# Index projection and index scores of a hybrid SSD / sparse-attention layer joined into one stage

## What is computed

```python
h = jnp.einsum('bld,de->ble', x, w_in)            # ... qi (8 x 64), ki (64), wi (8) are columns of it
s = jnp.einsum('bqhd,bld->bqhl', qi, ki_all) * IDX_DIM ** -0.5
score = jnp.einsum('bqh,bqhl->bql', wi * IDX_HEADS ** -0.5, jax.nn.relu(s))
score = jnp.where(admissible[None], score, -jnp.inf)
top_val, top_idx = lax.top_k(score, k_sel)
```

## Time and profile before

| | us |
|---|---|
| median of 3 runs | 3117.87 (3112.76 to 3118.03) |
| span of the profiled execution | 3115.3 |
| index part (both stages), in that execution | 0 to 452.4 |
| of it, projection of the index columns | 0 to 215.6 |
| of it, scores | 219.0 to 452.2 |

### The profile page before, as it was taken

One profiled execution on the slowest core, in us unless ns is written; L12 is line 12 of the kernel. 1 busy time (PEld: TensorE's weight loads), 2 busy tenths in 40 slices (PEclk: granted clock), 3 DMA queues, 4 the chain that ended last, 5 costly groups with the idle time before them and its releaser, 6 DMA issues. The chain is left out here.

```text
span 3115.3 us, 40926 instructions
## 1 busy us (share of the span) xinstructions
PE 2719.6 (87%) x15348; PEld 2279.6 (73%) x15398; DVE 2179.2 (70%) x3768; ACT 1100.6 (35%) x1970; POOL 634.8 (20%) x694
## 2 busy tenths in 40 slices
PE   6879969999998999996577775899999986599998
PEld 4667539999998888996465653667777765488886
DVE  2326999999999999997688855666666655344333
ACT  2215971112221212212544442555554443232222
POOL 0002002333333333433044532211111000000000
PEclk8869989999999999998699987999999998799999
DMA  5320015222225233346412415211110005522221
GB/s 183 134 83 1 1 58 170 87 89 88 87 87 189 88 102 95 97 142 218 177 41 68 122 45 169 72 41 41 31 31 28 21 20 167 186 93 98 92 81 48
DMA packets 177409, 286.03 MB, mean 92 GB/s; under 512 B 27834, under 2 KB 125890, under 8 KB 173382
## 3 DMA queue, kind: packets, MB, share of 16 engines
q1 hardware_dynamic: 157401, 220.56, 22.4%
q0 software_dynamic: 19824, 62.97, 5.4%
HBM read 177.77 MB, written 105.71 MB: 91 GB/s over the span
## 5 line engine op out<-in xcount | busy, mean ns | idle before, releaser
L705 DVE TENSOR_SCALAR_CACHE_REDUCE project_junk<-all_S,project_cand 128x528 bf16<-128x528 f32 (+7 forms) x256 | 370.0, 1445 | 4.8 <-DVE project_cand L730 4.7
L629 PE MATMUL PS<-project_wh,project_xh 128*128 128x256 f32 x1224 | 348.0, 284 | 8.6 <-POOL project_wl L675 5.7
L629 PE MATMUL PS<-project_xh,project_wh 128*128 128x384 f32 (+1 forms) x880 | 317.0, 360 | 37.9 <-DMA project_xl<-x_parts 37.9
L629 PE MATMUL PS<-project_wl,project_xh 128*128 128x256 f32 x1224 | 347.6, 284 | 0.0
L629 PE MATMUL PS<-project_wh,project_xl 128*128 128x256 f32 x1224 | 347.4, 284 | 0.0
L1601 DVE TENSOR_TENSOR attend_ptl<-PS,attend_pth 128x512 fp32r<-128x512 f32 x272 | 186.3, 690 | 186.9 <-ACT attend_pth L1539 186.0
L629 PE MATMUL PS<-project_xh,project_wl 128*128 128x384 f32 (+1 forms) x880 | 316.3, 359 | 0.0
L629 PE MATMUL PS<-project_xl,project_wh 128*128 128x384 f32 (+1 forms) x880 | 316.0, 359 | 0.0
L705 DVE TENSOR_SCALAR_CACHE_REDUCE project_tie<-all_S,project_cand 128x384 bf16<-128x384 f32 (+6 forms) x224 | 315.7, 1409 | 0.0
L675 POOL TENSOR_TENSOR project_wl<-project_raw,project_wh 128x1024 fp32r<-128x1024 f32 x80 | 201.6, 2541 | 240.4 <-ACT project_wh L642 240.4
L1539 ACT CAST attend_pth<-PS 128x512 fp32r<-128x512 f32 x272 | 157.8, 585 | 242.2 <-PE PS L1486 241.2
(11 more groups left out here) (309 smaller groups left out, 6026.8 us busy)
## 6 DMA issues: line engine op xcount, KB each, us to landing
project_raw<-in_w_in SPq DMA_DIRECT2D x80, 512.0 KB, 4.4
featT<-project_st POOLq DMA_DIRECT2D x66, 192.0 KB, 2.2
featT<-project_st POOLq DMA_DIRECT2D x44, 256.0 KB, 2.3
gate_s<-project_st POOLq DMA_DIRECT2D x68, 128.0 KB, 2.1
gate_a<-project_st POOLq DMA_DIRECT2D x68, 128.0 KB, 2.2
x_conv<-all_S SPq DMA_DIRECT2D x8, 1088.0 KB, 5.3
conv_x<-x_conv SPq DMA_DIRECT2D x8, 1088.0 KB, 6.6
ssd_zs<-gate_s SPq DMA_DIRECT2D x17, 512.0 KB, 4.4
```

The lines of the kernel that those rows point to most:

```text
L629: last = nc.tensor.matmul(PS[:, r % 8, 0:w], lhsT, rhs, start=(k == 0 and j == 0), stop=(k == KT - 1 and j == 2))
L705: v.tensor_scalar((junk, tie)[j % 2][:, 0:L], tile_scores(j), th, None, op, ALU.add, accum_out=into[:, j:j + 1]).then_inc(counted, 1)
```

## The change

The two stages become one, `stage_index`, with one list of steps that all engines walk through. What it does:

- The sample chunk is projected first, then the four prompt chunks (`CH`). Its queries go to a buffer of their own (`qsS`); `qs` shrinks to two chunks of 512 tokens in turn.
- A step is a `turn` (transposing one tile), one eighth of a block (`block`, three matmuls), `back`, `cache` (cached keys of one sequence) or `score` (one unit). The function `spread` deals the score units evenly over the steps of something else.
- While chunk 2, 3 or 4 of this order is projected (tokens 512 to 1023, 1024 to 1535, 1536 to 2047), the score units of the chunk before are dealt over its steps from the fourth on: 16, 64 and 96 units. The other 128 units (tiles 12 to 15) are dealt over the 8 cache steps and the 16 sample units, which come last.
- PSUM: turns use two banks (halves of one tile), projection blocks two instead of three, rows back one, scores three instead of eight.
- The cached keys are loaded when the last projection product is done, since they lie where the weights' parts were. The small parameters are loaded right behind the weights and transposed in the very first step.
- The copies of the queries by POOL are made once a head instead of once a unit.

The diff, cut to its core (what ACT and DVE do in each step is as before, in the order of the list):

```diff
+        CH = [CUTS[-1]] + CUTS[:-1]
...
+        def spread(a, u, first):
+
+            out, done = [], 0
+            for i, step in enumerate(a):
+                out.append(step)
+                upto = len(u) * max(i + 1 - first, 0) // max(len(a) - first, 1)
+                out += u[done:upto]
+                done = upto
+            return out
...
+        def project_steps(c):
+            turns = [("turn", order.index(t)) for t in tiles_of[c]]
+            return turns + [("block", c, f, k) for f in range(5) for k in range(KT)]
+        units, steps = [], [("par",)] + project_steps(0) + project_steps(1)
...
+        for c in range(2, NC):
+            us = score_steps(paired([i for t in tiles_of[c - 1] if t >= SEL0 for i in items(t)]))
+            a = project_steps(c)
+            backs = [("back", j) for j in ((0, 1) if c == 2 else (c - 1,))]
+            steps += spread(a[:1] + backs + a[1:], us, 3)
+            ready.append(len(units))
+        steps.append(("back", NC - 1))
+        late_items = paired([i for t in tiles_of[NC - 1] for i in items(t)])
+        sample_items = paired(items(ST))
+        a = [("cache", s) for s in range(NB)] + [("score", i) for i in sample_items]
+        for step in spread(a, [("score", i) for i in late_items], 0):
+            steps += score_steps([step[1]]) if step[0] == "score" else [step]
...
+                sp.dma_start(rows[NB * 3 + 4:, :], b.ins["conv_b"].unsqueeze(0)).then_inc(rows_in, 16)
+                for i in range(3, TILES + 1):
+                    load(i)
+                sp.wait_ge(proj, 5 * NC)
+                sp.wait_ge(x_st, 32 * NC)
+                sp.dma_start(kc[:], b.cache_kidx.rearrange("b (k p) d -> p (b k) d", p=P)).then_inc(kc_in, 16)
...
+                def turn(i):
+                    pe.wait_ge(x_in[i % 3], 16 * (i // 3 + 1))
+                    for j in range(2):
+                        wait(pe, x_lo, 2 * (i - 1) + j + 1)
...
+                def score(n):
+                    (t, c0, w), h = units[n]
+                    c = chunk_of[t]
+                    if n == first_of[c]:
+                        pe.wait_ge(q_lo, 8 * (c + 1))
+                        pe.wait_ge(k_lo, c + 1)
+                    wait(pe, relu_done, n - 2)
+                    out = PS[:, 5 + n % 3, 0:w]
```

More of the change, by code:

```diff
@@ new lines, in items, with paired @@
+        def items(t):
+            return [(t, c, w) for c, w in even_pieces(keys_of(t))]
+        def paired(some):
+            return [(item, h) for i in range(0, len(some), 2) for h in range(IH) for item in some[i:i + 2]]
+        def spread(a, u, first):
[6 more added lines that the diff above has]
+            return out
@@ new lines, in stage_index @@
+        steps.append(("back", NC - 1))
[4 more added lines that the diff above has]
+            steps += score_steps([step[1]]) if step[0] == "score" else [step]
+        last_on = {}
+        before = []
+        for n, (item, h) in enumerate(units):
+            before.append(last_on.get(item, -1))
+            last_on[item] = n
@@ L206, in stage_index_proj, with run, nothing @@
+        def run(par, turn, block, back, cache, score):
+            act = {"par": par, "turn": turn, "block": block, "back": back, "cache": cache, "score": score}
+            for step in steps:
+                act[step[0]](*step[1:])
+        def nothing(*_):
+            pass
         with nc.Block() as block:
@@ L292, in _ @@
+                run(par, turn, block, back, cache, score)
             @block.scalar
@@ new lines, in block @@
+                def block(c, f, k):
+                    if k < KT - 1:
+                        return
+                    n, (c0, w) = 5 * c + f, CH[c]
+                    act.wait_ge(proj, n + 1)
+                    if f < 4:
+                        if f == 0 and c >= 3:
+                            wait(act, sim_ready, ready[c - 2])
+                        for r in range(2):
+                            half = slice(r * ID, (r + 1) * ID)
+                            cp(q_of(c, f, r)[half], PS[half, 2 + n % 2, 0:w]).then_inc(q_hi, 1)
+                    else:
+                        cp(kdw[0:NR, c0:c0 + w], PS[0:NR, 2 + n % 2, 0:w]).then_inc(k_raw, 1)
+                        act.wait_ge(k_raw, c + 1)
+                        for r in range(2):
+                            end = cp(ks[r * ID:(r + 1) * ID, 0, c0:c0 + w], kdw[0:ID, c0:c0 + w])
+                        end.then_inc(k_hi, 1)
@@ new lines, in cache, with score @@
+                def cache(s):
+                    act.wait_ge(kc_turned, s + 1)
+                    act.wait_ge(x_st, 32 * NC)
+                    for r in range(2):
+                        end = cp(kiS[r * ID:(r + 1) * ID, 0, s, 0:PAST], PS[0:ID, s % 2, :])
+                    end.then_inc(kc_hi, 1)
+                def score(n):
+                    (t, c0, w), h = units[n]
+                    act.wait_ge(sim_ready, n + 1)
+                    wait(act, acc_done, n - 3)
+                    nc.scalar.activation(relu[:, n % 4, 0:w], PS[:, 5 + n % 3, 0:w], ACT.Relu, scale=ID ** -0.5
+                                         ).then_inc(relu_done, 1)
@@ L324, in _ @@
+                run(par, turn, block, nothing, cache, score)
             @block.vector
@@ new lines, in cache @@
+                def cache(s):
+                    dve.wait_ge(kc_hi, s + 1)
+                    if s == 0:
+                        for part in range(2):
+                            v.tensor_copy(kiS[:, part, :, PAST:LS], ks[:, part, SEQ:TOK].rearrange(
+                                "p (b t) -> p b t", b=NB)).then_inc(new_done, 1)
+                    for r in range(2):
+                        end = v.tensor_tensor(kiS[r * ID:(r + 1) * ID, 1, s, 0:PAST], PS[0:ID, s % 2, :],
+                                              kiS[0:ID, 0, s, 0:PAST], ALU.subtract)
+                    end.then_inc(kc_lo, 1)
```

430 lines of the change are left out of this document (197 added, 233 removed).

## The result

| | before | after |
|---|---|---|
| median of 4 runs, us | 3115.32 (3112.49 to 3118.03) | 3065.73 (3056.91 to 3068.49) |
| span of the profiled execution | 3115.3 | 3064.5 |
| start of the big projection | 452.5 | 401.5 |
| from there to the end of the span | 2662.8 | 2663.0 |

The ratio is 0.9839, 95% interval 0.9821 to 0.9856: 49.6 us less. The last line of the table says that all of it was won in the index part, and that what follows kept its length in these two executions.

A forecast was written before the change was run, and what follows sets the result against it. The index part was bound by PE in projections, then DVE in prompt scores; seven pieces, each timed by its slowest engine, moved its end from 452.4 to 403 us, saving 49: forecast 3069 us, range 3040 to 3102.

The forecast's parts named there:

- Start, first product at 26: Start of the index part: sample tile first, one tile turned instead of four; first product at 26 instead of 32.2 us.
- Sample chunk, 23.6 us at the lower level: Projection of the sample chunk: 120 matmuls of 128 columns at the lower clock, 23.6 us as before, end 50.
- Chunk 1, gap 11.5, end 92: Tiles 0 to 3, nothing to overlap: gap of 11.5 us (bounds 9 and 14), 30.3 us of products, end 92.
- Chunk 2, gap 12.3, end 141: Second prompt chunk: gap 12.3 us, products 30, 16 score units on PE 6.5; 49 us in all, end 141.
- Cache keys, 9.5 us to DVE's next work, 297: Behind the last product: wait for the cached keys' transfer, 9.5 us with first transposes and roundings, to 297.
- Last part, 102.5 us: 128 late units over 8 cache steps (34 us by DVE) and 16 sample units (68.5 by PE): 102.5 us, to 399.5.
- Each is last in its own half: Last part: DVE limits the cache steps, PE the sample units; three PSUM banks and four buffers can't even that out.
- POOL's copies at nothing: Sample half: POOL's query copies, 11 us in all, cost nothing under DVE's slack of 9.6; without cover up to 11.
- Rival (a), more gain: Chunk gaps filled, last part evened out to 95 us, sample chunk partly at higher clock: 3050 us; chance 0.19.
- Rival (b), jitter with three banks: In-order queues jitter: sample half 82 instead of 68.5 us, cache steps and two chunks lose too: 3099 us; chance 0.18.
- Rival (c), the clock: Short PE stops drop the granted clock to 1.2 GHz; the whole last part there gives 3149 us; chance 0.07.
- Rival (d), no overlap: Queues block each other, parts add up as before, only start and barrier are saved: 3105 us; chance 0.04.

The follow-up runs named there:

- both rebalancing runs: Against the changed kernel: 16 late units ahead of the first cache step, start 400.6 us; two late units per cache step, seven per sample unit, 402.8; unedited 401.5.

## Why the prediction was right

The forecast was 3069 us and the median is 3065.7. The likeliest case came true, in its mechanism and nearly in its sum; by the steps:

- **What bounds the kernel.** The prediction called PE full in slices 1 to 3 of the strip, where it stands at 6, 8 and 7 tenths; full is right for the products alone, and PE idles at the start and between chunks. The sum was made from the stretches and not from the strip, so nothing hangs on it.
- **The question, when the big projection starts.** Right: the rest kept its length to 0.2 us. That it was so near is luck; in the twelve other executions of changed kernels it took 2655.5 to 2665.4 us against 2662.8 before.
- **Start, first product at 26.** 26.3. The small loads landed at 16.99 and not near 20, so the cover over the new first step was wider than thought.
- **Sample chunk, 23.6 us at the lower level.** 24.3 us. The value was right, and the reason I gave for keeping it ("although back to back") was half of it: back-to-back 128-column products did not raise the clock in 24 us, but entered at the higher pace they kept it for the 12.6 us that they need in two executions, and lost it after 2 us in a third. The trace of before had a fourth case that the prediction passed over: its sample chunk was entered at 0.11 us a product and fell to 0.21 after 0.8 us.
- **Chunk 1, gap 11.5, end 92.** Gap 10.5, end 91.0. It would have been 88 where the clock stays up in the gap, as in three of the thirteen rows.
- **Chunk 2, gap 12.3, end 141.** Gap 14.2, end 140.9: the gap is 1.9 longer, the products with their units are 35.7 instead of 36.5, and chunk 1 had given 1 us.
- **Chunk 3, gap 13.3, end 207.** Gap 13.1, products with units 50.6 for 52.5; end 204.6.
- **Chunk 4, gap 14.5, 80.5 in all, end 287.5.** 79.8 in all; end 284.4. PE is full and DVE close behind (58.9 of 65), as predicted.
- **Cache keys, 9.5 us to DVE's next work, 297.** From 284.4 to 294.9: 10.5 us, the hole that was forecast.
- **Last part, 102.5 us.** 105.1, to the last score at 400.0. Here two terms are mis-sized in opposite directions. The cache half is 31.5 for 34: DVE makes 38 score units in it and not 42, the others are still in the buffers when PE begins its first sample unit, so these 2 us only moved on. The sample half is 73.6 for 68.5. PE takes 71.2 us for it, and a sample unit with its 5.3 late ones 4.4 us and not 4.3. The widths are as priced (67 of its 86 late units are 512 wide, 0.44 us on the mean), and with six banks such a step takes 59.6 / 14 = 4.26 us, so what the price left out is PE's waits with three banks. Behind PE's last matmul the last relus and multiply-adds take 2.3 us more; I had put these into the drain, which is 1.5 us instead of 3.5.
- **"Each is last in its own half."** Right as read from the stretches; the hope that follows from it, a gain by moving units, is not (both rebalancing runs).
- **POOL's copies at nothing.** Right, shown by tripling them.
- **Rival (a), more gain.** Not seen: gaps, last part and sample clock stayed. Its mechanisms are real only in part: the sample clock is worth 11 us where it holds, the gaps 2, evening out the last part nothing so far.
- **Rival (b), jitter with three banks.** Seen with three at some 2 us in the sample half, not at the 13.5 that it was priced at there. My reason against it, that PE leads by some 4 us of DVE work, does not hold, since with two banks the same reasoning gave 2 to 8 us and 29 came. Three banks was right by one bank.
- **Rival (c), the clock.** Granted 1.00 in chunks 3 and 4 and in the sample half, and also with two banks and four times the waits. In the cache half it was 0.88, under the 0.9 that was named as a sign of being wrong, and 0.95 from the last product to 400 us; DVE is the last engine in the cache half, so no time is seen to be lost by it.
- **Rival (d), no overlap.** Excluded; undoing the overlap costs 30 us in the chunks and 19 in the last part.

The misses of single terms (-3 in chunks 3 and 4, +1 at the cache keys, +2.6 in the last part, -2 in the drain) cancel in part, so the sum is better than its terms, and that part of its precision is luck. The clock ahead of chunk 1 could have put the start some 3 us earlier, too.

## What to carry to other kernels

Where one stage fills one engine and the next fills another, price the fusion piece by piece with the pace of each engine per step, and ask at what time the first untouched stage starts; such a sum held within 2 us over 400. Moving work between pieces pays only the price on the engine that is last where it is taken away, and costs the price on the engine that is last where it is put. A busy share of 100% does not say that an engine's waits are free: compare the length of a step that repeats, with one buffer fewer and with many more, and the granted clock in the same stretch. An unchanged total can hide a gain and a loss. And before a gain is put down to an edit, look where in the chain it appears: 3 us of one run here stood ahead of everything that the edit touched.

## What the runs showed of the hardware

- A stream of 128-column products does not reach the higher level of the clock by itself in 24.3 us. Entered at the higher pace, it kept it for its 12.6 us in two executions and lost it in two, after 2 us and, in the kernel before, after 0.8 us. The granted clock's column read 1.00 from 20 to 52 us of the changed kernel while products started every 0.21 us; the pace of the instructions was the surer sign.
- With the same steps ahead of it, the granted clock fell in the gap before chunk 1 in some executions and not in others, which is worth 1.9 us in the products behind it.
- Of PSUM banks between PE and ACT, in a loop that mixes units of 2 us with units of 0.46, two lose 22 us of 117, and three lose 2.0 us over fourteen steps of 4.3 us against six. With six, PE's idle time gathered ahead of the first sample unit (3.5 us, and 6.3 with eight relu buffers), and the clock fell to 0.50 over it in all three executions.
- GpSimd's eight small copies took 1.9 to 4.3 us beside a busy VectorE, for 1.37 us beside a VectorE with little to do, and VectorE kept its pace (2.08 us for three multiply-adds, with them and without).
